# Some modulation chunks of a two-block transformer kernel go from TensorE to VectorE, with a TensorE sum over partitions one step later

## The chip, the cores and the metric

One core of a Trainium2 chip runs the whole program in one launch. The time is the device time of that core in microseconds, from the first instruction to the last; lower is better.

## What is computed

Batch 1, 256 tokens, width 1024, all in float32. `first_block` has two layers, each with a token mixer (sparse attention over an index, forgetting attention, two gated branches) and a convolutional FFN of inner width 2816. `second_block` adds two layers of five gated branches. Only the modulation of the first block matters here:

```python
for l in range(DEPTH):                      # DEPTH = 2
    mod = c @ mod_w[l] + mod_b[l]           # c: 1 x 1024, mod_w[l]: 1024 x 6144
    sh1, sc1, g1, sh2, sc2, g2 = [m[:, None, :] for m in jnp.split(mod, 6, axis=-1)]
    h = _rmsnorm(x, norm1_g[l]) * (1.0 + sc1) + sh1
    x = x + g1 * _mixer(h, ...)
    h = _rmsnorm(x, norm2_g[l]) * (1.0 + sc2) + sh2
    x = x + g2 * _conv_ffn(h, w_up[l], conv_w[l], conv_b[l], w_down[l])
```

Each `mod` is a row vector times a 1024 x 6144 matrix: six groups g of 1024 columns, cut into four parts of 256 columns. A chunk is one such part, 1024 x 256 weights, 1 MB. Two layers have 48 chunks.

## The kernel before

**Planning.** `plan()` writes a list of steps in one order. Each engine goes through this same list and issues what it has to do for each step, so the list is at once the order of every engine's queue. Weights come as 1 MB chunks through a ring of five buffers (`RING`), one DMA each on SP's queue; SP waits for the chunk five places earlier to be released. A weight chunk has two blocks of eight 128 x 128 tiles. ScalarE copies each block to `w_hi` (L1649, rounded to fp32r), VectorE writes the rest `w_lo` (L2042), and TensorE makes three products per tile: L1351, L1352, L1357 (L1389, L1390, L1395 for token-major outputs). There are six slots for split blocks (`SPLIT`). `split_to(upto)` on ScalarE and `split_to(behind)` on VectorE (one block fewer) stand ahead of each step's own work.

**A modulation chunk on TensorE** (`mod`, L1435): eight float32 matmuls with a 128 x 32 stationary operand, in four column groups, so that four partial rows arise at partitions 0, 32, 64 and 96. ScalarE copies them to `modacc` (L1698). With part 3 of a group, ScalarE writes the four rows of the group to HBM (`mod_rows`, L1703); `modload` reads them back feature-major (L1710), waiting first for the write to have arrived; `modsum` on VectorE (L2047, L2144) adds the four rows and the bias.

**A modulation chunk on VectorE** exists for two chunks at the start (`first_mod` with by_vector): eight chained instructions over 128 x 256 (L2119, L2121, L2122), each scaling by one column of `c` and adding to `modacc`. What is left, a sum over 128 partitions, is done there by small matmuls (`modred`).

**Who calls.** `some_mod()` first calls `reduce_mod()` (which adds `modsum` for a group already loaded, then `modload` for a group just completed) and then takes one chunk from the queue, in the order g = 2, 4, 3, 5 of layer 0 and g = 0, 1, 2, 4, 3, 5 of layer 1. In layer 0 it is called twice in the projections, once after the fox queries, after each odd gate tile (`gate1`, j = 1 to 15), after each of the first y1 groups as long as the next chunk isn't of g = 5, after odd `up` steps, and after each of the eight outputs `dn` of the down projection. `gap_mod()` puts one chunk on either side of the norm that follows. In the step list of layer 0 the chunks are: (4,3) after gate j = 9, then (3,0), (3,1), (3,2) after j = 11, 13, 15 and (3,3) in y1; (1,2,0) ahead of the down projection, then (1,2,1) to (1,2,3), (1,4,0) to (1,4,3), (1,3,0) after dn 0 to dn 7, and (1,3,1), (1,3,2) around the norm of layer 1.

**The down projection.** `dn` j takes 22 tiles (66 matmuls); VectorE then adds the bank to x (L2413), ScalarE squares x (`stat`, L1683). After the last one TensorE sums the squares (L1413, L1416), `root` takes the logarithm and exponent on ScalarE (L1688, L1690), and VectorE finishes the root and the norm.

**Sparse attention next to the gates.** `tp` turns the probabilities, which VectorE and ScalarE copy in turn out of the bank (L2355, L1843); `pv` (L1526) multiplies with the values; `no` (L2363, L2047) divides on VectorE; `lg` (L2328) is VectorE's pass over the next tile's logits.

## Time and profile before

| | |
|---|---|
| three runs | 1539.85, 1541.74, 1541.89 us; median 1541.74 |
| the profiled execution | 1542.8 us, of which the span is 1541.0 us |
| TensorE busy | 1496.3 us, 97% |
| VectorE busy | 1143.7 us, 74% |
| ScalarE busy | 833.4 us, 54% |
| mean granted TensorE clock | 0.993 |
| DMA | 290.5 MB, mean 189 GB/s |

In the profile PE is TensorE (PEld its weight loads), DVE VectorE, ACT ScalarE, POOL GpSimd, SP SyncE. L12 is line 12 of the kernel. In a timeline row stand start, duration, engine, line, operation, output and inputs, and in brackets the idle time ahead of it with what ended it; durations of TensorE matmuls overlap, so their starts are to be read.

### The profile page before, as it was taken

How to read it: one execution, taken by the hardware profiler on the slowest of the kernel's cores; microseconds unless marked ns; L12 is line 12 of the kernel's file. 1: busy time of each engine (PE TensorE's matmuls, PEld its weight loads, DVE VectorE, ACT ScalarE, POOL GpSimd, SP SyncE). 2: the span in 40 equal slices, each digit the busy share in tenths (PEclk: the TensorE clock that was granted, in tenths of full speed). 3: DMA queues.
4: the chain of work that ended last, by engine and by line, in shares of the span. 5: the costliest groups of instructions: out<-in, count | busy, mean ns of one | idle time of the engine just before them, and what ended most of it. 6: DMA issues, size and time to landing. Idle time of an engine off the chain costs nothing.

```text
span 1541.0 us, 31309 instructions
## 1 busy us (share of the span) xinstructions
PE 1496.3 (97%) x12608; PEld 1433.5 (93%) x12608; DVE 1143.7 (74%) x2202; ACT 833.4 (54%) x1509; POOL 31.4 (2%) x36
## 2 busy tenths in 40 slices
PE   6999999999999999999999999999999999999997
PEld 4898898999998999989999989999999999999997
DVE  5758566888646586769996678878966988888774
ACT  3655545655435646446555655645555754645453
POOL 0000001000000000010001000000000000000000
PEclk9999999999999999999999999999999999999998
DMA  9654555676776452454545543443446444444430
GB/s 393 251 216 184 202 223 192 219 275 247 275 272 252 168 214 87 157 196 165 179 179 194 219 164 113 169 185 138 154 152 246 150 154 163 167 163 141 169 129 28
DMA packets 47840, 290.51 MB, mean 189 GB/s; under 512 B 9992, under 2 KB 12296, under 8 KB 13136
## 3 DMA queue, kind: packets, MB, share of 16 engines
q1 hardware_dynamic: 38880, 280.83, 49.0%
q10 hardware_dynamic: 8816, 7.67, 1.5%
q8 instruction: 101, 1.65, 0.4%
q14 instruction: 43, 0.35, 0.1%
HBM read 286.09 MB, written 2.39 MB: 187 GB/s over the span
## 4 chain that ended last, share of the span: by engine, by line
PE 57%; DVE 1%; ACT 1%; DMA 0%; issue 0%; DVEq 0%; ACTq 0%
PE bank L1351 17%; PE bank L1357 16%; PE bank L1352 16%; PE bank L1601 2%; PE sums L1526 1%; PE sums L1416 1%; PE bank L1390 1%; PE bank L1395 1%; PE bank L1389 1%; PE bank L1508 1%; PE bank L1499 1%; DMA mem_x<-mem_t 0%; DVE w_lo L2042 0%; ACT w_hi L1649 0%; PE bank L1533 0%
## 5 line engine op out<-in xcount | busy, mean ns | idle before, releaser
L1351 PE MATMUL bank<-h_hi,w_hi 128*128 128x256 f32 x2256 | 632.8, 288 | 8.9 <-ACT h_hi L1746 3.7
L1352 PE MATMUL bank<-h_hi,w_lo 128*128 128x256 f32 x2256 | 622.3, 283 | 0.0
L2042 DVE TENSOR_TENSOR w_lo<-ring,w_hi 128x1024 fp32r<-128x1024 f32 x436 | 523.4, 1222 | 106.4 <-ACT w_hi L1649 103.8
L1357 PE MATMUL bank<-h_lo,w_hi 128*128 128x256 f32 x2256 | 575.9, 283 | 0.0
L1649 ACT ACTIVATE w_hi<-ring 128x1024 fp32r<-128x1024 f32 x436 | 449.2, 1054 | 131.4 <-PE bank L1357 130.9
L1351 PEld LDWEIGHTS bank<-h_hi,w_hi 128*128 128x128 f32 x2256 | 432.8, 192 | 22.9 <-issue 17.9
L1352 PEld LDWEIGHTS bank<-h_hi,w_lo 128*128 128x128 f32 x2256 | 433.0, 192 | 0.6 <-issue 0.5
L1357 PEld LDWEIGHTS bank<-h_lo,w_hi 128*128 128x128 f32 x2256 | 405.2, 192 | 0.0
L1351 PE MATMUL bank<-a_hi,w_hi 128*128 128x256 f32 x352 | 99.6, 283 | 1.0 <-DVE w_lo L2042 0.7
L1352 PE MATMUL bank<-a_hi,w_lo 128*128 128x256 f32 x352 | 98.3, 279 | 0.0
L1357 PE MATMUL bank<-a_lo,w_hi 128*128 128x256 f32 x352 | 98.2, 279 | 0.0
L1389 PE MATMUL bank<-w_hi,h_hi 128*128 128x256 f32 (+1 forms) x304 | 86.6, 289 | 3.9 <-ACT h_hi L1746 2.9
L1390 PE MATMUL bank<-w_lo,h_hi 128*128 128x256 f32 (+1 forms) x304 | 85.7, 286 | 0.0
L1883 ACT ACTIVATE conv_a<-bank,sm 128x256 f32<-128x256 f32 x44 | 24.8, 564 | 105.2 <-PE bank L1357 105.2
L1395 PE MATMUL bank<-w_hi,h_lo 128*128 128x256 f32 (+1 forms) x304 | 81.7, 287 | 0.0
L1351 PE MATMUL bank<-y_hi,w_hi 128*128 128x256 f32 x288 | 79.3, 280 | 0.0
L1352 PE MATMUL bank<-y_hi,w_lo 128*128 128x256 f32 x288 | 78.8, 278 | 0.0
L1357 PE MATMUL bank<-y_lo,w_hi 128*128 128x256 f32 x288 | 75.7, 281 | 0.0
L1944 ACT ACTIVATE sig<-bank 128x256 f32<-128x256 f32 x80 | 30.3, 379 | 78.1 <-PE bank L1357 77.5
L1351 PEld LDWEIGHTS bank<-a_hi,w_hi 128*128 128x128 f32 x352 | 66.1, 188 | 4.7 <-issue 3.3
L1389 PEld LDWEIGHTS bank<-w_hi,h_hi 128*128 128x128 f32 x304 | 59.6, 196 | 7.2 <-issue 5.9
L1352 PEld LDWEIGHTS bank<-a_hi,w_lo 128*128 128x128 f32 x352 | 66.2, 188 | 0.0
(336 smaller groups left out, 2345.7 us busy)
## 6 DMA issues: line engine op xcount, KB each, us to landing
ring<-weights SPq DMA_DIRECT2D x266, 1024.0 KB, 4.9
pos_bias<-scratch ACTq DMA_DIRECT2D x4, 512.0 KB, 5.6
x<-x_t ACTq DMA_DIRECT2D x1, 1024.0 KB, 6.9
scratch<-line ACTq DMA_DIRECT2D x1, 1024.0 KB, 5.6
mem_x<-mem_t ACTq DMA_DIRECT2D x1, 1024.0 KB, 6.7
mem_second<-mem_t ACTq DMA_DIRECT2D x1, 1024.0 KB, 6.2
out_t<-x SPq DMA_DIRECT2D x2, 512.0 KB, 2.6
co<-const SPq DMA_DIRECT2D x1, 462.0 KB, 7.2
```

Of the source, the lines that this page charges most:

```text
L1351: pe.matmul(to, WH[:, b % SPLIT, o, :], hi[:, k, :], start=(i == 0), stop=False)
L1352: pe.matmul(to, WL[:, b % SPLIT, o, :], hi[:, k, :], start=False, stop=False)
L1357: last = pe.matmul(to, WH[:, b % SPLIT, o, :], lo[:, k, :], start=False, stop=(i == n - 1))
L1389: pe.matmul(o, q, WH[:, s:s + m.n, k, :], start=(k == 0), stop=False)
L1390: pe.matmul(o, q, WL[:, s:s + m.n, k, :], start=False, stop=False)
L1395: last = pe.matmul(o, q, WH[:, s:s + m.n, k, :], start=False, stop=(k == KD - 1))
L1416: m = pe.matmul(sums[:, 0:S], ones, hb[:, k, :], start=(st.n is None and k == 0), stop=(k == KD - 1))
L1601: m = pe.matmul(to[:, (2 * g + s) * P:(2 * g + s + 1) * P], k[half, g, s * P:s * P + P], q[half, g, t * P:t * P + P], start=True, stop=True)
L1649: act.activation(WH[:, b % SPLIT], ring_half(b), ACT.Copy).then_inc(w_hi, 1)
L1883: act.activation(to[:, st.j % 3, :], bank[u.bank][:, 0:S], ACT.Identity, scale=ss(("conv_w", st.l, 2), c), bias=ss(("conv_b", st.l), c)).t ...
L1944: act.activation(sig2[:, st.j % 4, :], bank[st.ps.bank][:, 0:S], ACT.Tanh, scale=0.5).then_inc(taken[st.ps.bank], 1)
L2042: ve.tensor_tensor(WL[:, b % SPLIT], ring_half(b), WH[:, b % SPLIT].bitcast(F32), ALU.subtract).then_inc(w_lo_v, 1)
```

## The change

`some_mod()` gets a flag by_vector. It is set after gate tiles with j > 8 of layer 0, and after dn with j < 6 of layer 0. A chunk taken with the flag is made by VectorE as eight chained instructions, and takes no bank and no step of TensorE. The sum over the 128 partitions follows in a new step `modrow`, which `some_mod()` puts into the list at its next call, ahead of the next chunk: one float32 matmul with a 128 x 128 block of ones, so that every partition holds the sum, and ScalarE copies it to `modacc` scaled by 0.25 (four rows of it are added later). When the row completes a group, `some_mod()` returns without taking a chunk. VectorE now also waits ahead of such a chunk for the previous group's rows to have been written to HBM. In the diff the three engine parts at the end are TensorE's, ScalarE's and VectorE's, in this order.

```diff
+BY_VECTOR = 6
...
+    def mod(l, g, part, by_vector=False):
         p.chunks.append(("mod", (l, g, part)))
-        st = p.add("mod", chunk=len(p.chunks) - 1, l=l, g=g, part=part, ps=p.full_bank(),
-                   n=p.count("mod_rows") if part == 3 else p.counts.get("mod_rows", 0), after=state["parts"])
+        n = p.count("mod_rows") if part == 3 else p.counts.get("mod_rows", 0)
+        more = dict(v=p.count("mod_v"), eng="vector") if by_vector else dict(ps=p.full_bank(), after=state["parts"])
+        st = p.add("mod", chunk=len(p.chunks) - 1, l=l, g=g, part=part, n=n, **more)
+        if by_vector:
+            state["row"] = st
+            return
         state["parts"].append(st.ps)
         if part == 3:
             state["summed"] = (l, g)
+
+    def mod_row():
+        st, state["row"] = state["row"], None
+        if st:
+            row = p.add("modrow", l=st.l, g=st.g, part=st.part, n=st.n, v=st.v, ps=p.full_bank(), after=state["parts"])
+            state["parts"].append(row.ps)
+            if st.part == 3:
+                state["summed"] = (st.l, st.g)
...
-    def some_mod(n=1):
+    def some_mod(n=1, by_vector=False):
         reduce_mod()
+        mod_row()
+        if state["summed"]:
+            return
         for _ in range(min(n, len(queue))):
             l, g, part = queue.pop(0)
-            mod(l, g, part)
+            mod(l, g, part, by_vector)
...
     def gap_mod():
-        if queue and not state["summed"]:
+        if queue and not state["summed"] and not state["row"]:
             mod(*queue.pop(0))
...
             if j % 2 and queue and queue[0] > (0, 9, 9) and len(queue) > 4 or j % 2 and l == 0:
-                some_mod()
+                some_mod(by_vector=l == 0 and j > 8)
...
             if queue and queue[0][1] != 5:
                 some_mod()
+            else:
+                mod_row()
...
             ps = fm("dn", dn[j], j=j, l=l).ps
-            some_mod()
+            some_mod(by_vector=l == 0 and j < BY_VECTOR)
...
+            def modrow(st):
+                to = claim(st.ps)
+                pe.wait_ge(mod_v, st.v + 1)
+                pe.matmul(to[:, 0:256], ones, modacc[:, st.part, :], start=True, stop=True).then_inc(ready, 1)
...
+            def modrow(st):
+                wait_ready(act, st.ps)
+                act.activation(modacc[:, st.part, :], bank[st.ps.bank][:, 0:256], ACT.Copy, scale=0.25).then_inc(
+                    taken[st.ps.bank], 1)
+                if st.part == 3:
+                    for u in st.after:
+                        wait_taken(act, u)
+                    act.dma_start(mod_rows.ap()[st.n], modacc[0:97:32, :, :]).then_inc(mod_row_out, 16)
...
             def mod(st):
                 if st.eng != "vector":
                     return
+                if st.n is not None:
+                    ve.wait_ge(mod_row_out, 16 * st.n)
```

## Rows read from the trace of the kernel before

**Rows 1.** Profile page: busy time by engine, share of the span, instructions.
```profile
PE 1496.3 (97%) x12608; PEld 1433.5 (93%) x12608; DVE 1143.7 (74%) x2202; ACT 833.4 (54%) x1509; POOL 31.4 (2%) x36
```

**Rows 2.** Timeline of PE around a modulation chunk of the down projection.
```profile
438.41 0.28 PE L1357 MATMUL bank<-a_lo,w_hi 128*128 128x256 f32 x1
438.62 1.07 PE L1435 MATMUL bank<-ring,c_wide 128*32 128x256 f32 x16
439.62 0.39 PE L1351 MATMUL bank<-a_hi,w_hi 128*128 128x256 f32 x1
```

**Rows 3.** Timeline of PE at the root: float32 sums with ones, two records a matmul.
```profile
466.32 0.70 PE L1413 MATMUL sums<-mean,co 128*128 128x256 f32 x2
466.85 0.59 PE L1416 MATMUL sums<-h_val,co 128*128 128x256 f32 x2
```

**Rows 4.** Timeline of DVE at the start: one modulation chunk by VectorE.
```profile
13.40 0.35 DVE L2119 TENSOR_SCALAR modacc<-ring,sm 128x256 f32<-128x256 f32 x1 [4.42 <-DMA ring<-weights]
17.31 0.15 DVE L2047 TENSOR_TENSOR modv<-bank,sm 128x2 f32<-128x2 f32 x1
```

**Rows 5.** Timeline of DVE beside the gates, 167 to 176 us.
```profile
167.29 0.19 DVE L2363 RECIPROCAL stats<-stats 128x8 f32<-128x8 f32 x1
170.01 0.69 DVE L2047 TENSOR_TENSOR o_tm<-sums,stats 128x512 f32<-128x512 f32 x1 [2.53 <-PE sums L1526]
171.09 0.69 DVE L2047 TENSOR_TENSOR o_lo<-bank,o_hi 128x512 fp32r<-128x512 f32 x1 [0.38 <-ACT o_hi L1854]
...
175.40 0.42 DVE L2355 COPY probs_t<-bank 128x256 f32<-128x256 f32 x1
```

**Rows 6.** Timeline of PE, same place: last gate matmul, first `pv`.
```profile
175.56 0.28 PE L1357 MATMUL bank<-h_lo,w_hi 128*128 128x256 f32 x1
175.97 0.52 PE L1526 MATMUL sums<-v_a,probs_t 128*128 128x64 f32 x3
```

**Rows 7.** Timeline of DVE: the longest idle beside gate j = 13; ahead of wo1.
```profile
195.36 0.69 DVE L2047 TENSOR_TENSOR o_tm<-sums,stats 128x512 f32<-128x512 f32 x1 [4.58 <-PE sums L1526]
...
234.88 0.48 DVE L2408 SCALAR_TENSOR_TENSOR x<-bank,modv,x 128x256 f32<-128x256 f32 x1 [5.42 <-PE bank L1357]
```

**Rows 8.** Timeline of DVE in the down projection, dn 3 to dn 5.
```profile
438.73 0.48 DVE L2413 SCALAR_TENSOR_TENSOR x<-bank,modv,x 128x256 f32<-128x256 f32 x1 [5.01 <-PE bank L1357]
...
441.40 0.81 DVE L2047 TENSOR_TENSOR modv<-modv 128x16 f32<-128x16 f32 x2
...
448.10 3.48 DVE L2042 TENSOR_TENSOR w_lo<-ring,w_hi 128x1024 fp32r<-128x1024 f32 x3
```

**Rows 9.** Timeline of ACT: row write at dn 6; copy and root behind dn 7.
```profile
459.92 0.50 ACTq L1703 DMA_DIRECT2D mod_rows<-modacc  x1
460.46 0.42 ACT L1683 ACTIVATE h_val<-x 128x256 f32<-128x256 f32 x1 [0.65 <-ACT modacc L1698]
...
468.34 0.36 ACT L1698 ACTIVATE modacc<-bank 128x256 f32<-128x256 f32 x1
...
470.23 0.47 ACT L1688 ACTIVATE guess<-sums,co 128x256 f32<-128x256 f32 x1 [0.91 <-PE sums L1416]
```

**Rows 10.** DMA queues in 463.92:464.42, 4.0 to 4.5 us after that row write's issue.
```profile
q10 hardware_dynamic: 1, 0.00, 0.1%
```

**Rows 11.** DMA queues in 168.38:168.88, 1.0 to 1.5 us after an earlier row write's issue.
```profile
q10 hardware_dynamic: 8, 0.02, 12.3%
```

**Rows 12.** Windows of 2 us: stretch, busy PE, PEld, DVE, ACT, POOL, PEclk, DMA share, GB/s.
```profile
476.00:478.00 2.00, 2.00 (x11) 2.00 (x11) 2.00 (x7) 1.18 (x3) 0.00 (x0) 0.50 1.00 422
...
680.00:682.00 2.00, 1.57 (x13) 1.60 (x14) 1.82 (x6) 1.17 (x4) 0.00 (x0) 1.00 1.04 438
```

**Rows 13.** Timeline of PE: its work after idle at two norms.
```profile
469.06 1.13 PE L1416 MATMUL sums<-h_val,co 128*128 128x256 f32 x4 [1.61 <-ACT h_val L1683]
...
474.05 0.36 PE L1389 MATMUL bank<-w_hi,h_hi 128*128 128x256 f32 x1 [2.00 <-ACT h_hi L1746]
...
680.43 0.36 PE L1351 MATMUL bank<-h_hi,w_hi 128*128 128x256 f32 x1 [1.86 <-ACT h_hi L1746]
```

More of the change, by code:

```diff
@@ L188, in plain @@
         return p.matrix([tile_cols(name, lead, [(c0 + P * j, P)], rows) for j in range(n)])
-    state = dict(parts=[], summed=None, loaded=None, added={}, all_by_pe={})
-    def mod(l, g, part):
+    state = dict(parts=[], summed=None, loaded=None, added={}, all_by_pe={}, row=None)
+    def mod(l, g, part, by_vector=False):
         p.chunks.append(("mod", (l, g, part)))
-        st = p.add("mod", chunk=len(p.chunks) - 1, l=l, g=g, part=part, ps=p.full_bank(),
-                   n=p.count("mod_rows") if part == 3 else p.counts.get("mod_rows", 0), after=state["parts"])
+        n = p.count("mod_rows") if part == 3 else p.counts.get("mod_rows", 0)
[4 more added lines that the diff above has]
+            return
         state["parts"].append(st.ps)
@@ L1625, in from_h @@
                 linear([(claim(st.ps)[:, 0:S], st.subs)], XH, XL)
-            do = dict(bias=bias, root=root, norm=norm, mem_again=mem_again, mod=mod, modred=modred, tm=tm, tr=tr,
+            do = dict(bias=bias, modrow=modrow, root=root, norm=norm, mem_again=mem_again, mod=mod, modred=modred, tm=tm, tr=tr,
                       cum=cum, idx=idx, qkf=from_h, gate1=from_h, lg=lg, tp=tp, pv=pv, ot=ot, y1=y1, wo1=wo1, up=up,
@@ L2010, in hgn @@
                 act.activation(hb[:, 6:8, :], hb[:, 6:8, :], ACT.Exp, scale=-0.5).then_inc(hg_guess, 1)
-            do = dict(setup=setup, bias=bias, mod=mod, modload=modload, stat=stat, root=root, norm=norm, mem_again=mem_again, load_mem=load_mem, tm=tm, decay=decay, idx=idx, tr=tr, decay2=decay2,
+            do = dict(setup=setup, bias=bias, mod=mod, modrow=modrow, modload=modload, stat=stat, root=root, norm=norm, mem_again=mem_again, load_mem=load_mem, tm=tm, decay=decay, idx=idx, tr=tr, decay2=decay2,
                       qkf=qkf, gate1=gate1,
```

## The prediction

> **What bounds the kernel now.** I began with the page's busy times: TensorE is busy 97% of the span, VectorE 74% [rows 1]. So a microsecond taken from TensorE's queue is a microsecond won, as long as nobody makes TensorE wait; and VectorE has 26% to give, if the free time lies where the work is put. The questions are local: how long TensorE spends on one modulation chunk, how long VectorE would, and what ends VectorE's idle time in the two stretches that the change touches. For these I read the timelines of PE and DVE there, then ACT and the DMA queues at the end of the down projection, because the change also moves the steps that follow a chunk.
>
> **How many chunks.** Following `some_mod` through the new code, not all flagged calls take a chunk. At the gates, j = 9 takes (4,3) by VectorE. At j = 11 its row is added, the group is complete, and the call returns without a chunk. j = 13 and 15 take (3,0) and (3,1). That is three, not four. In the down projection dn 0, 1, 2 take (2,1), (2,2), (2,3) of layer 1, dn 3 adds the last row and returns, dn 4 and 5 take (4,0) and (4,1): five, not six. Eight chunks are moved, and each return shifts all later chunks by one place: (3,2) and (3,3) of layer 0 are made by TensorE during y1; at dn 6 and dn 7 stand (4,2) and (4,3) by TensorE; and one chunk of g = 5 slides into the up stage of layer 1.
>
> **TensorE's side.** A chunk occupies it from 438.41 + 0.12 (the pitch of the matmul before) to the next start at 439.62: 1.09 us [rows 2]. The new row is a float32 matmul of 128 x 128 on 128 x 256. The trace has that very form, the sums at the root: from 466.32 to 466.85, 0.53 us [rows 3]; with 0.09 us for the change of kind, as ahead of 438.62, it is 0.62 [rows 2]. I take 0.575. So 8 x (1.09 - 0.575) = 4.1 us less, with 3.8 and 4.5 as its ends.
>
> **VectorE's side.** One chunk takes from 13.40 to 17.31, 3.91 us [rows 4].
>
> *Down projection.* After each dn VectorE adds to x, splits two or three blocks (three take 3.48 us), now and then does `modsum`, and then waits 5.0 us for TensorE [rows 8]. With the chunk it needs 0.40 + 3.42 + 3.91 = 7.7 us where three blocks are split; TensorE's period becomes 66 x 0.1165 + 0.575 = 8.3 us. It fits with half a microsecond to spare, and the row of each chunk, which TensorE asks for after the next dn, is there in time. Only after dn 5 there is `modsum` too (from 441.40 to about 442.4, 0.95 us): 8.7 us against 8.2, so the row of (4,1) holds TensorE for 0.45 us. Bounds: 0 (the splits can run ahead), 1.5 (0.3 at each of five rows). The ring buffer of a VectorE chunk is released some 6 us later than now, and SP's loads queue behind it; I placed the loads one by one and each still lands before its split, so nothing there.
>
> *Gates.* Here the chunk (4,3) comes right ahead of the reciprocal at 167.29, so it runs from there to 171.20. Queued behind it on VectorE are the reciprocal and the division `o_tm`, now at 170.01 after an idle of 2.53 [rows 5]: it would start at 171.45, 1.44 late. The idle of 0.38 and what else the semaphores cost ahead of `o_lo` at 171.09 takes some back, leaving 0.97. From there to the copy of the probabilities at 175.40 VectorE has no idle time, and that copy is just what TensorE needs at 175.97: the last gate matmul starts at 175.56, so 0.29 us of the gap is already a wait [rows 6]. TensorE would arrive 1.09 earlier and leave 0.97 later. The saving of this chunk is gone and 0.97 lost on top; as a stall beyond the TensorE sum it is 0.97 + 1.09 = 2.05 us. Bounds: 0.6 (if the logit passes catch up 1.4 us more) and 3.0. (3,0) falls into the idle of 4.58 us ahead of 195.36 [rows 7] and costs nothing. (3,1) delays the first y1 sums by some 2.5 us; TensorE's own chunks (3,2), (3,3) give that back by the third y1 pair, and ahead of the first sum of wo1 VectorE is idle for 5.42 us [rows 7]. Nothing.
>
> **What moves at the end of the down projection.** Today the last rows of group (1,4) are written with dn 6, at 459.92 [rows 9], and loaded behind dn 7, one period of 8.9 us later; by then the write has arrived. In the new plan (4,3) is made after dn 7, so its row write and, right behind the last squares, its `modload` stand on ScalarE's queue ahead of the logarithm of `root`. `modload` first waits for the write to have arrived. Queued behind it: L1688 and with it VectorE's root, the norm of layer 1 and TensorE. In the time of the old trace: the copy at 468.34, the write issued at 468.82, the squares 0.75 later (0.65 us of idle as at 460.46), so TensorE's sum would let the logarithm start at 470.98 instead of 470.23. It starts when both this and the load's issue are done. How long does a row write take? Ten are in the trace. With the queues nearly empty all eight packets moved 1.0 to 1.5 us after the issue [rows 11]; with weights filling them, which is the state at the end of the down projection, the last packet of the write at 459.92 moved 4.0 to 4.5 us after it [rows 10]. With 4.3: 468.82 + 4.3 + 0.4 for the load's issue = 473.5, against 470.23 now: 3.3 us. `modsum`, 0.95 us [rows 8], no longer stands ahead of VectorE's root, and I take a quarter of a microsecond back for it: 3.0 us. Bounds: 0.5 (write in 1.25 us; then only the late squares count) and 5.0 (write in 6.3 us, behind three loads).
>
> The rule on this is in the Trainium skill, DMA: Bandwidth & Descriptors, in its part on the fixed cost: about 2 us for any DMA, mostly the receipt of the write. Taken as it stands the logarithm would be 0.7 us late instead of 3.0. This trace disagrees where the queues are full [rows 10].
>
> **The sum.** -4.1 (TensorE) + 2.05 (gates) + 0.45 (row after dn 5) + 3.0 (root of layer 1) = +1.4 us. The chunk that slides into the up stage is in the count already. Added to the median, 1541.74 + 1.4 = 1543.1 us; the profiled run, 1542.8 with a span of 1541.0, would become about 1544.2 with a span of 1542.4. The difference of span and median is 0.7 us, which is in the range.
>
> **The rivals.**
>
> 1. *The forecast, +1.4.* For it: the place on ScalarE's queue is certain, the DMA state is that of [rows 10]. Chance 0.46.
>
> 2. *The write is quick.* Loads are issued later than now because ring buffers are held longer, and the write meets a gap. Then the root costs 0.5 to 0.7 and the sum is -1.0: 1540.7 us. Against it: the loads delayed by VectorE's last chunk bunch just there. The page's 2 us for a DMA is this case. Chance 0.17.
>
> 3. *All of VectorE's work hides and the write is quick:* -4.1 + 0.5 = -3.6, 1538.1 us. It needs the gate stretch to have slack that I don't see in [rows 5, 6]. Chance 0.10.
>
> 4. *The write waits behind the loads (slower).* At the root three chunks of 1 MB are due at once, since the buffers of (4,1), (4,2) and (4,3) come free within a few microseconds. If the write arrives more than 6 us after its issue, the root costs 4.7 or more and the sum passes +3.1; at 7.5 us it is +4.6: 1546.3 us. For it: the ring is fuller than today. Chance 0.17.
>
> 5. *The clock falls beside the gates.* TensorE would idle there for 0.97 + 1.09 + 0.29 = 2.3 us in one piece. After 1.86 us of idle, at 680.43, the granted clock stayed at 1.00, 2.4 GHz; after 1.61 and, a few microseconds later, 2.00 us of idle at the root of layer 1 it was 0.50, 1.2 GHz, for some 2.6 us [rows 12, 13]. If it falls here too, half of 2.6, 1.3 us, is lost: +2.7, 1544.4 us. The Trainium skill has this rule in TensorE: Matmul & The Clock Gate, in its part on oscillation: idle gaps put the clock to half. At the root the clock falls already, so a longer idle there costs little more. Chance 0.10.
>
> That the plan moves ten chunks and not eight would be -1.0 more; the code speaks against it, and it is in the width.
>
> **How the numbers follow.** What the measurement can tell from no change is about 0.2%, 3.1 us: below 1538.7 is faster, above 1544.8 slower. Rival 3 and the best end of 2 are faster: 0.10. Rival 4, and the worse end of 1 and 5, are slower: 0.24. The rest, 0.66, is the same. Range: from -2.8 (rivals 2 and part of 3) to +5.0 (rival 4 almost whole), 1538.9 to 1546.7.
>
> **What the profile after would show.** Right: 8 groups of L2122's kind more on VectorE and a new PE line with 16 float32 records; 64 matmuls, 128 records, fewer at the chunk line; an idle of 2.3 us of PE ahead of the `pv` behind gate j = 10, ended by the copy of VectorE; VectorE idle of about 0.5 us per dn where 5.0 stood; ScalarE idle for 2 to 3 us ahead of the logarithm behind the last dn of layer 0, and PE idle there of about 5 us instead of 2.00. Wrong: no idle at either place; a wait for `w_lo` or for weights' DMA inside the down projection, which would mean that the ring or VectorE is the bound; or the logarithm starting right after TensorE's sum.

## The result

The kernel after takes 1549.17 us, median of 15 runs (1543.94 to 1551.33), beside 1543.22 us for the kernel before in as many. The ratio is 1.0032, with an interval of 1.0023 to 1.0040: 3.5 to 6.2 us slower, 4.9 us at its middle; the two medians differ by 5.95 us. The forecast was +1.4 us and 1543.1 us, its range ended at 1546.7. So the sign was right, the size was not, and the time left the band that was called "the same". Of the 6.1 us between forecast and time, 1.5 us lie in the base: the forecast was added to 1541.74 us, the median of three runs, and fifteen runs of the kernel before give 1543.22.

The profiled execution of the kernel after took 1544.88 us (span 1543.1), one of its quickest; three further traces of it had spans of 1548.5, 1550.1 and 1551.1 us, two further ones of the kernel before 1542.7 and 1542.2.

Profile page of after, busy time by engine, beside [rows 1]:

```profile
PE 1492.4 (97%) x12496; PEld 1434.4 (93%) x12496; DVE 1174.7 (76%) x2266; ACT 832.6 (54%) x1509; POOL 31.6 (2%) x36
```

TensorE is busy for 3.9 us less and VectorE for 31 us more, as planned. TensorE's lines there, instructions, busy time and idle time before them:

```profile
L1459 PE MATMUL bank<-ring,c_wide 128*32 128x256 f32 x608 | 43.5, 411 | 14.5 <-DMA ring<-weights 14.5
L1448 PE MATMUL bank<-modacc,co 128*128 128x256 f32 x16 | 5.0, 393 | 1.0 <-DVE modacc L2157 0.9
```

Sixteen records of the new row step, two each, are eight moved chunks and not ten, as the prediction counted them.

**Beside the gates.** Timeline of PE in after; shown are the rows with idle time ahead of them, and a row step with its successor (the place of [rows 6]):

```profile
171.51 0.38 PE L1370 MATMUL bank<-h_hi,w_hi 128*128 128x256 f32 x1 [1.00 <-DVE o_lo L2080]
175.65 0.63 PE L1550 MATMUL sums<-v_a,probs_t 128*128 128x64 f32 x4 [1.00 <-DVE probs_t L2390]
179.22 0.60 PE L1448 MATMUL bank<-modacc,co 128*128 128x256 f32 x2
179.65 0.55 PE L1550 MATMUL sums<-v_a,probs_t 128*128 128x64 f32 x4
...
182.17 0.66 PE L1550 MATMUL sums<-v_a,probs_t 128*128 128x64 f32 x4 [1.35 <-ACT probs_t L1876]
```

Three waits, 3.35 us, where the kernel before has 0.13 us ahead of its first `pv` (175.56 + 0.28 to 175.97, [rows 6]) and 0.07 ahead of the third. In the whole stretch from 117 to 255 us TensorE is idle for 5.51 us, before for 2.36: 3.15 us more. Timeline of DVE ahead of the first two, beside [rows 5]:

```profile
169.54 0.48 DVE L2157 SCALAR_TENSOR_TENSOR modacc<-ring,sm,modacc 128x256 f32<-128x256 f32 x1
169.94 0.20 DVE L2398 RECIPROCAL stats<-stats 128x8 f32<-128x8 f32 x1
170.17 0.69 DVE L2080 TENSOR_TENSOR o_tm<-sums,stats 128x512 f32<-128x512 f32 x1
170.78 0.68 DVE L2080 TENSOR_TENSOR o_lo<-bank,o_hi 128x512 fp32r<-128x512 f32 x1
...
175.08 0.42 DVE L2390 COPY probs_t<-bank 128x256 f32<-128x256 f32 x1
```

The chunk (4,3) ends at about 169.9, and reciprocal, division and `o_lo` follow without idle time. The next gate tile needs the bank that `o_lo` reads: that is the first wait. Together with the second, ahead of `pv`, it is the idle time that was forecast as one piece of 2.3 us. The third was not forecast. Timeline of ACT:

```profile
180.64 0.38 ACT L1718 ACTIVATE modacc<-bank 128x256 f32<-128x256 f32 x1
181.12 0.51 ACTq L1723 DMA_DIRECT2D mod_rows<-modacc  x1
181.74 0.38 ACT L1876 ACTIVATE probs_t<-bank 128x256 f32<-128x256 f32 x1 [0.72 <-ACT modacc L1718]
```

The row's copy and the issue of the row write of group (4) stand on ScalarE's queue ahead of a copy of probabilities that TensorE is waiting for. In the kernel before, this write is issued some 14 us earlier, at 167.38 (its packets are [rows 11]). Not all of the 1.35 us is the write's: experiments 4 to 6 issue no write here, and a wait of 0.68 us stands at this place, because TensorE arrives earlier.

**Down projection and root.** Timeline of PE in after, the rows with idle time (beside [rows 2] and [rows 13]):

```profile
453.82 0.67 PE L1448 MATMUL bank<-modacc,co 128*128 128x256 f32 x2 [0.93 <-DVE modacc L2157]
455.13 1.07 PE L1459 MATMUL bank<-ring,c_wide 128*32 128x256 f32 x16 [0.64 <-DMA ring<-weights]
...
468.57 1.13 PE L1435 MATMUL sums<-h_val,co 128*128 128x256 f32 x4 [2.40 <-ACT h_val L1707]
...
471.97 1.07 PE L1459 MATMUL bank<-ring,c_wide 128*32 128x256 f32 x16 [1.27 <-DMA ring<-weights]
476.37 0.55 PE L1408 MATMUL bank<-w_hi,h_hi 128*128 128x256 f32 x1 [3.33 <-ACT h_hi L1779]
```

Timeline of ACT, same place (beside [rows 9]):

```profile
467.53 0.52 ACTq L1736 DMA_DIRECT2D mod_rows<-modacc  x1
468.10 0.72 ACT L1707 ACTIVATE h_val<-x 128x256 f32<-128x256 f32 x2 [0.68 <-ACT modacc L1731]
472.39 0.36 ACTq L1743 DMA_DIRECT2D modv<-mod_rows  x1
472.80 0.47 ACT L1712 ACTIVATE guess<-sums,co 128x256 f32<-128x256 f32 x1 [3.98 <-DMA mod_rows<-modacc]
```

Row write, squares, `modload`, logarithm, in the order that the prediction read out of the plan. The write is issued at 467.53, the load could go at 472.39: 4.86 us, and 5.20, 5.25 and 5.15 us in the other three traces of this kernel. The write's eight packets moved 3.5 to 5.0 us after its issue.

**Where the time goes.** The table has the time between starts of TensorE's matmuls behind idle times that both kernels have, in us, for all traces of the two. The first matmul of layer 0 comes at 33.8 to 36.2 us in all of them.

| stretch of TensorE | before (3 traces) | after (4 traces) |
|---|---|---|
| layer 0 to the first logits of the forgetting attention (117 us) | 81.70, 82.66, 82.08 | 81.88, 82.00, 83.10, 83.10 |
| to the second norm (255 us): gates, y1, wo1 | 138.09, 139.59, 138.08 | 139.24, 139.23, 140.72, 140.72 |
| to the sums of the root (469 us): up, down | 214.05, 215.53, 214.04 | 213.69, 214.34, 214.21, 214.15 |
| root of layer 1 (474 us) | 4.99, 4.99, 4.99 | 7.80, 8.16, 8.19, 8.10 |
| to 551 us | 76.90, 75.42, 76.90 | 77.50, 77.00, 76.93, 77.12 |
| to the second norm of layer 1 (680 us) | 129.48, 129.49, 129.46 | 129.49, 130.99, 130.99, 130.97 |
| to the second block's first norm (894 us) | 213.92, 213.43, 212.98 | 212.99, 212.99, 214.45, 215.53 |
| to the end | 646.65, 646.60, 647.52 | 646.75, 647.79, 646.73, 646.74 |
| sum | 1505.8, 1507.7, 1506.1 | 1509.3, 1512.5, 1515.3, 1516.4 |

The same step of about 1.5 us turns up in many lines, in both kernels. It is TensorE's clock. Windows of 2 us around the second norm (stretch, busy PE, PEld, DVE, ACT, POOL, PEclk, DMA share, GB/s), first of after:

```profile
254.00:256.00 2.00, 1.12 (x9) 1.15 (x10) 1.82 (x6) 1.33 (x3) 0.00 (x0) 0.97 1.00 422
256.00:258.00 2.00, 2.00 (x11) 2.00 (x11) 2.00 (x6) 1.15 (x4) 0.00 (x0) 0.50 1.03 434
258.00:260.00 2.00, 2.00 (x14) 2.00 (x13) 1.90 (x5) 1.43 (x4) 0.00 (x0) 0.68 1.00 410
```

and of the kernel before, in its third trace:

```profile
256.00:258.00 2.00, 1.69 (x14) 1.72 (x15) 1.90 (x5) 1.17 (x4) 0.00 (x0) 1.00 1.00 422
258.00:260.00 2.00, 2.00 (x19) 2.00 (x19) 2.00 (x6) 1.33 (x3) 0.00 (x0) 1.00 1.02 430
```

Behind the same idle of 1.86 us the granted clock is 0.50, 1.2 GHz, in the one and 1.00, 2.4 GHz, in the other. Such a fall costs 1.5 to 1.7 us over work, and it comes or stays away from execution to execution.

### The profile page after: what moved, and what is told of

The parts are those of the page before. It is cut to its first block, busy times and chain, and to the rows that moved or that the text cites. A ratio compares the mean times of both kernels' runs of the same rounds, so it can differ in the third digit from the quotient of the medians.

```text
span 1543.1 us, 31154 instructions
## 1 busy us (share of the span) xinstructions
PE 1492.4 (97%) x12496; PEld 1434.4 (93%) x12496; DVE 1174.7 (76%) x2266; ACT 832.6 (54%) x1509; POOL 31.6 (2%) x36
## 4 chain that ended last, share of the span: by engine, by line
PE 58%; DVE 2%; ACT 1%; issue 0%; DVEq 0%; ACTq 0%
PE bank L1370 17%; PE bank L1376 16%; PE bank L1371 16%; PE bank L1625 2%; PE sums L1550 1%; PE sums L1435 1%; PE bank L1409 1%; PE bank L1414 1%; PE bank L1408 1%; PE bank L1532 1%; PE bank L1523 1%; DVE w_lo L2075 0%; PE bank L1557 0%; PE bank L1638 0%; DVE macc L2080 0%
```

## The experiments

All medians are of 5 to 15 runs each unless a single run is named; a ratio is that to the kernel before on the same chip, with its interval, and 0.1% is 1.5 us. A "+3.5 us" is worked out from the ratio and can differ from the difference of two medians.

**1. The kernel after once more**, unchanged.

> The changed kernel again, unchanged, for a second trace. Its fifteen times fell into two groups, 1544 to 1545.5 us with a mean granted clock of 0.991 to 0.995, and 1549 to 1551 us with 0.988 to 0.992. Theory A (the clock of TensorE): the second group differs from the first by a longer stretch at 1.2 GHz, some 9 to 10 us more at half clock for 4.6 us lost, at one place where TensorE has just idled; the root of layer 1 is the candidate (0.5 from 474 to 480 us in the first trace). A trace of the second group then shows PEclk 0.5 in more windows and otherwise the same rows. Rival B (DMA): the second group waits longer for weights or for the row write, PEclk as before. A trace of 1544 to 1545 us again would tell neither.

1550.33 us, 1.0044 (1.0031 to 1.0057). The loss is real. Its trace has the same three waits beside the gates, 1.31 us of waiting for weights at 458 us, and 17.1 us of time lost to the clock before 1520 us, counted as the length of each 2 us window times (1 - PEclk); the first trace of after has 8.5, those of before have 6.8, 10.2 and 10.3. Theory A is the nearer one, though not at one place: more clock is lost than in the first trace near 30 us, at the root and near 900 us, and the clock also falls at 558 us. The third and fourth traces lost 15.4 and 17.1 us.

**2. Only the three chunks beside the gates.**

```diff
-BY_VECTOR = 6
+BY_VECTOR = 0
```

> The changed kernel with the flag off in the down projection; three chunks beside the gates by VectorE remain. Theory: the gates alone cost about 1.1 us (stalls of 1.0, 1.0 and 1.35 us of TensorE at 170 to 182 us against 3 x 0.5 saved), so ratio to before about 1.0007, and no wait for the row write at the root of layer 1. Rival (the gates carry the loss, by a clock that falls there in some runs): ratio 1.002 to 1.003 and two groups of times as with the whole change.

> Only the three chunks beside the last gates of layer 0 go by VectorE ((4,3), (3,0), (3,1)); all chunks of the down projection stay on TensorE. The run of the same kernel came out at 1548.64 us, 1.0032 of the kernel before, while its traced span shows only 3 stalls of 1.0, 1.0 and 1.35 us against 1.5 us saved. Theory A (the stalls are all there is, and the rest was the clock of few executions): the median lands near +1.5 to +2.5 us, ratio 1.001 to 1.0017. Theory B (the stalls beside the gates are followed by a lower granted clock or by waits for weights in a good part of the executions): +4 to +5.5 us again, ratio 1.0026 to 1.0036, and a trace with more than 8.5 us of clock lost before 1520 us or idle time of TensorE ended by weights in the down projection.

> One more execution of the kernel with only the three gate chunks by VectorE, for its trace. Its two traces so far had a wait for weights at 432 us (0.89 and 1.43 us) and 6.8 us of clock lost before 1520 us each, no more than the kernel before (6.8, 10.3 and 10.3). If the +4.7 us of its timed executions is clock lost near the gates in a part of them, one of its traces should sooner or later show a low clock between 160 and 260 us: here in about half the cases. If it shows none and again a wait for weights near 432 us, the waits behind the gates are the steady part of the loss and the clock's part stays open.

The edit takes the flag off the down projection, and the third of the three is a single run. 1548.64 us, 1.0032 (1.0020 to 1.0044), and again 1547.93 us, 1.0030 (1.0018 to 1.0042): +4.6 to +4.9 us where the forecast had 0.5 for these chunks (2.05 less 3 x 0.515). All three traces have the waits of 1.0, 1.0 and 1.35 us. In two of them the stretch from 117 to 255 us takes 1.14 us longer for it; in the second it takes 2.60 us longer, because TensorE also waits 1.40 us for weights at 217 us. Then there is a wait that nobody had on the list, in the down projection, where the steps and their order are those of the kernel before. Timeline of PE in its second trace:

```profile
434.33 1.07 PE L1459 MATMUL bank<-ring,c_wide 128*32 128x256 f32 x16 [1.43 <-DMA ring<-weights]
```

It is 0.89, 1.43 and 1.47 us. No ring buffer is released late here; the load itself is slow, 6.8, 7.3 and 7.4 us from issue to landing, where the same load takes 4.7 to 5.0 us in seven traces of kernels with the same steps there, the kernel before and experiments 3 and 4 among them. Why, the runs don't show. Together the steady waits are +2.0 to +2.6 us. The three traces take 4.0 us more than those of before on the mean, and that is 2.4 us of these waits, 0.5 for the wait at 217 us in one of three, and 1.1 us of clock. For the ratios, taken from other executions, the part of the clock isn't measured. In the third trace the clock is full beside the gates and 1.7 us are lost at 258 to 262 us, behind the second norm.

**3. Only chunk (4,3) beside gate 9.**

```diff
-                some_mod(by_vector=l == 0 and j > 8)
+                some_mod(by_vector=l == 0 and j == 9)
```

(and `BY_VECTOR = 0`)

> Only chunk (4,3) beside gate 9 of layer 0 goes by VectorE, its row added at j = 11; all others stay on TensorE, later chunks one place later. Theory A (the two stalls of 1.0 us behind it and the one of 1.35 us behind the row write are the whole loss of this place): 3.35 minus 0.52 saved, less 1.1 for the chunk that slides out of the gates into an idle place: +1.5 to +2.8 us, ratio 1.001 to 1.0018. Theory B (each stall there also brings a stretch of low clock): +3.5 to +5 us, ratio 1.0023 to 1.0032. If it comes out within 1 us of no change, the loss of the three-chunk version lies with (3,0) and (3,1).

1546.85 us, 1.0022 (1.0012 to 1.0032): +3.4 us. The one chunk brings all three waits. It was also expected that a chunk slides out of the stretch; it doesn't, (3,3) is made in y1 either way. Without that term the waits give 3.15 - 0.71 = +2.4 us (0.71 by experiment 5). In the trace the stretch to 255 us takes 142.26 us: that is +2.4 and a fall of the clock at 118 to 124 us. Its root of layer 1 is 1.0 us longer too, 5.99 us, though the steps there are those of before: VectorE waits 0.90 us for the load of group (1,4), which lands 5.6 us after its issue. The ratio lies between A and B, and the interval reaches into both.

**4. No chunk (4,3) beside the gates**, that is (3,0), (3,1), (3,2) at j = 11, 13, 15, and none in the down projection.

```diff
-                some_mod(by_vector=l == 0 and j > 8)
+                some_mod(by_vector=l == 0 and j > 10)
```

(and `BY_VECTOR = 0`)

> Beside the gates alone, j = 11, 13, 15 by VectorE, chunk (4,3) by TensorE, the down projection as before the change. Theory: the stalls of 1.0, 1.0 and 1.35 us come from chunk (4,3) and its row, so they are gone, and three swaps save 1.5 us: ratio 0.999, mean 5 to 6 us below that of the gates-only kernel. Rival (the extra 4 us of the gates-only kernel over what its trace shows are chance or from somewhere else): the difference of the means is 1.1 + 1.5 = 2.6 us.

1543.97 us, 1.0001 (0.9989 to 1.0013). The waits of 1.00, 1.00 and 1.35 us are gone (one of 0.68 is left), and so are the wait for weights at 432 us and the loss of experiment 2; the gain of 1.5 us that was expected lies within the interval but isn't shown.

**5. No group's last part by VectorE, so no call returns empty and nothing is shifted.** Eight chunks, as in after.

```diff
-                some_mod(by_vector=l == 0 and j > 8)
+                some_mod(by_vector=l == 0 and j > 10)
...
-            some_mod(by_vector=l == 0 and j < BY_VECTOR)
+            some_mod(by_vector=l == 0 and j < BY_VECTOR and queue[0][2] != 3)
```

> The change with the last part of each group left to TensorE: beside the gates the flag holds for j > 10, in the down projection for chunks of parts 0 to 2. Again eight chunks go to VectorE, but no call returns without a chunk, so every later chunk, row write and load stands where it stood before the change, and VectorE has none between gate tiles 9 and 10. Theory (the loss is from where the moved steps stand, not from VectorE's work as such): no stall at 170 to 182 us, no wait of the logarithm for the row write, 8 x 0.5 us saved, some 3 to 4 us under before, ratio 0.9975 to 0.9985. Rival (VectorE's work in itself costs, through the ring or the splits): ratio at or above 1.000.

1542.92 us, 0.9999 (0.9990 to 1.0008): the 5 us are gone, but the gain of 2 to 4 us that was expected isn't there. The stretch of the gates takes 136.56 us, 1.53 less than 138.09, though TensorE is idle in it for 2.97 us instead of 2.36, by a wait of 0.68 us for a copy of ScalarE: (1.53 + 0.61) / 3 = 0.71 us saved by a chunk. The rest of the gain ends in the down projection. Timeline of PE, rows with idle time:

```profile
436.35 0.67 PE L1448 MATMUL bank<-modacc,co 128*128 128x256 f32 x2 [0.77 <-DVE modacc L2157]
...
455.49 1.78 PE L1459 MATMUL bank<-ring,c_wide 128*32 128x256 f32 x16 [1.62 <-DMA ring<-weights]
```

The matmuls behind the second wait take 1.78 us where they take 1.07 elsewhere: the granted clock is 0.50 at 456 to 458 us, and another 1.7 us are lost. At the root TensorE's chunk waits 2.01 us for its weights, in the place of the idle time of 2.00 us.

**6. Six chunks: as 5, but in the down projection only up to dn 3.**

```diff
-            some_mod(by_vector=l == 0 and j < BY_VECTOR)
+            some_mod(by_vector=l == 0 and j < 4 and queue[0][2] != 3)
```

> A version that keeps only the chunks with idle time of VectorE around them and with no row write in the way: (3,0), (3,1), (3,2) beside the last gates, (2,1), (2,2), (4,0) in the down projection, six in all, each group's last part on TensorE, so nothing is shifted at the root. Saved: 6 x 0.515 = 3.1 us. Theory A (the loss of the eight-chunk variant without shifts, 0.9999, came from the waits for weights at the end of the down projection, 1.62 and 2.01 us, because the last ring buffers were held by VectorE): ratio 0.9975 to 0.9990. Theory B (what TensorE saves is given back at the next idle place or by the clock, whatever the chunks): 0.9995 to 1.0010.

1541.71 us, 0.9987 (0.9978 to 0.9995): 0.8 to 3.4 us faster than the kernel before, the only one here whose interval lies below 1. Its trace has no wait for weights in the down projection, only the wait of 0.78 us for VectorE's chunk at 434.97. Up and down take 213.12 us, 0.93 less, with 2.70 us of idle time instead of 1.78: (0.93 + 0.92) / 3 = 0.62 us saved by a chunk. That the ring buffers held late are the difference to 5 fits the two traces; two chunks fewer are moved as well, and the two aren't told apart.

**7. Only the down projection's chunks.**

```diff
-                some_mod(by_vector=l == 0 and j > 8)
+                some_mod()
```

> The changed kernel with the flag off beside the gates; five chunks in the down projection by VectorE remain. Theory: the down projection saves 1.1 us by its end, the root of layer 1 then costs 3.6 (the logarithm behind the arrival of the row write), so 1.5 to 2.5 us over before in the trace; if the two groups of times belong to the root, they are here too and the ratio is 1.0015 to 1.003. Rival (the loss is at the gates): ratio at or below 1.000.

1546.10 us, 1.0019 (1.0010 to 1.0027), +2.9 us; with experiment 2 the parts give 7.5 us, against 4.9 and 6.8 us for the whole. Up and down take 211.99 us, 2.06 less than 214.05: just the forecast -5 x 0.515 + 0.45 = -2.1, though by other terms: -5 x 0.62, +0.94 for the row behind dn 5, +0.42 for weights, +0.79 for late squares and -1.09 for the chunk that leaves the stretch are -2.0 (all below). The root takes 8.15 us, as in after.

**8. Only the shift, no work for VectorE.** The kernel before; behind dn 3 of layer 0 no chunk is taken.

```diff
-            some_mod()
+            if l or j != 3:
+                some_mod()
```

> The kernel before with every chunk on TensorE; the only edit: no chunk is taken behind dn 3 of layer 0, so each later chunk stands one place later, and the row write of group (1,4) and its load stand on ScalarE's queue ahead of the logarithm of the root of layer 1, as in the kernel after. No VectorE work, no other saving. Theory A (the root is the place of the loss, and the clock makes it more): layer 1 starts 2.5 to 3.6 us later by the idle time alone, less 0 for savings (the one chunk slides into the up stage), and the granted clock at the root stays low for longer, 1.7 us more: +3 to +5 us, ratio 1.002 to 1.0034. Theory B (the wait costs only what the idle time shows, the clock falls there in any case): +2 to +3.2 us, ratio 1.0013 to 1.002. Theory C (without the late loads of VectorE's chunks the write arrives quickly): under +1 us, ratio below 1.0007.

1547.14 us, 1.0023 (1.0013 to 1.0033), +3.5 us. Shifting steps, with nothing else changed, costs 3.5 of the whole change's 4.9 us. Timeline of ACT:

```profile
470.07 0.50 ACTq L1704 DMA_DIRECT2D mod_rows<-modacc  x1
470.62 0.72 ACT L1684 ACTIVATE h_val<-x 128x256 f32<-128x256 f32 x2 [0.66 <-ACT modacc L1699]
475.03 0.40 ACTq L1711 DMA_DIRECT2D modv<-mod_rows  x1
475.47 0.47 ACT L1689 ACTIVATE guess<-sums,co 128x256 f32<-128x256 f32 x1 [4.13 <-DMA mod_rows<-modacc]
```

4.96 us from write to load without any late buffer of VectorE. The root takes 7.97 us.

**9. The same shift, with the load behind the root.** The call of `reduce_mod()` that followed the down projection of layer 0 now stands in `norm`, behind `root(...)`.

```diff
             root(i, kind)
+        if late_load:
+            reduce_mod()
         if mods:
...
         x_stats = stats([], "x", down)
-        reduce_mod()
+        if l == L1 - 1:
+            reduce_mod()
```

> The kernel with the shifted chunks and no VectorE work (1.0023), with one more edit: the load of group (1,4) stands behind the root of layer 1 on ScalarE's queue, so nothing at the root waits for the row write. If the wait for the write is the loss: the excess falls from 3.6 us to 0 to +1 us, ratio 0.9998 to 1.0007, and the idle times at the root are 1.6 and 2.0 us again. Rival (the later squares and the chunk shifted into the root are the loss): +2 to +3.5 us, ratio 1.0013 to 1.0023.

1543.11 us, 1.0004 (0.9995 to 1.0013). ACT:

```profile
471.96 0.50 ACTq L1707 DMA_DIRECT2D mod_rows<-modacc  x1
472.51 0.72 ACT L1687 ACTIVATE h_val<-x 128x256 f32<-128x256 f32 x2 [0.66 <-ACT modacc L1702]
474.14 0.47 ACT L1692 ACTIVATE guess<-sums,co 128x256 f32<-128x256 f32 x1 [0.91 <-PE sums L1420]
474.65 0.42 ACT L1694 ACTIVATE guess<-guess 128x256 f32<-128x256 f32 x1
477.68 0.36 ACTq L1714 DMA_DIRECT2D modv<-mod_rows  x1
478.14 0.38 ACT L1702 ACTIVATE modacc<-bank 128x256 f32<-128x256 f32 x1 [3.08 <-DMA mod_rows<-modacc]
478.42 0.90 ACT L1750 ACTIVATE h_hi<-h_val,modv 128x256 fp32r<-128x256 f32 x2
```

The write took even longer, 5.72 us. The logarithm doesn't wait for it any more and starts when TensorE's sum is there. But the load still holds ScalarE's queue: the copy `h_hi` of the norm starts 1.87 us after VectorE's `h_val` (476.55, timeline of DVE), against 0.52 us in the kernel before (472.88 and 473.40), and the root takes 6.08 us against 4.99. The squares are 0.8 us late (an idle of 2.38 where 1.61 was). The chunk that slides out of the stretch saves 1.1 us, so +0.8 us is left, and the ratio gives +0.6. Here the trace is that of the slowest of eleven runs, 1548.67 us, with 15.3 us of clock lost; the place is read from it, not the time. So most of the loss at the root is the load's wait for the write ahead of the logarithm; the rival, late squares and the shift as such as the whole loss, has fallen.

**10. The kernel after with that load behind the root.**

> The whole change, but the load of group (1,4) stands behind the root's logarithm and exponent on ScalarE's queue instead of ahead of them. Theory (the wait for the row write costs 3 us at the root, and sets off the longer stretch at half clock): the logarithm starts as soon as TensorE's sum ends, about 2.5 us earlier, the idle of TensorE ahead of layer 1 goes from 3.3 back to about 1 to 2 us, and the time falls by 2.5 to 3 us, to a ratio of about 1.0005 to 1.001 to before, in one group of times. Rival: the norm waits for something else (the row write only hid it), and the time stays within 1 us of the whole change.

1546.33 us, 1.0022 (1.0011 to 1.0032), against 1.0032 and 1.0044 of after; the intervals overlap, so it is the trace that shows the gain. The idle ahead of the norm's first matmul falls from 3.33 to 1.17 us, the root from 8.06 (mean of four) to 5.68. The gates' 1.14 us are left, and 0.69 at the root, where the load waits for the write as in 9; the rest of the +3.4 us isn't located.

**11 and 12. The price of idle time at the root by itself.** The kernel before; two and then six copies of the sums on ScalarE ahead of the logarithm, chained by a semaphore.

```diff
+                if st.i == 2:
+                    for i in range(2):
+                        act.activation(guess[:], sums[:, 0:S], ACT.Copy).then_inc(delayed, 1)
+                        act.wait_ge(delayed, i + 1)
```

> The kernel before, with two more operations of ScalarE (a copy of the sums, chained by a semaphore, some 0.5 us each as the logarithm is) ahead of the logarithm of the root of layer 1; nothing else. It prices idle time of TensorE at this place by itself: about 1.0 us more. Theory A (a longer idle there makes a second stretch of low clock more likely): the time is 1.5 to 3 us up, ratio 1.001 to 1.002. Theory B (the idle costs itself alone): +1.0 us, ratio 1.0004 to 1.0009.

> As the kernel with two added operations of ScalarE ahead of the logarithm of the root of layer 1, but six: about 3.0 us more of idle time of TensorE, as the forecast had it for the kernel after. Theory A (the long idle costs a further stretch of low clock): +4.5 to +5.5 us, ratio 1.003 to 1.0036, and the trace shows 3.4 us of clock lost or more between 460 and 490 us instead of 1.7. Theory B (the idle costs itself alone): +3.0 us, ratio 1.0017 to 1.0022, 1.7 us of clock lost there.

Two: 1546.46 us, 1.0015 (1.0005 to 1.0025), +2.3 us; the trace has 0.58 us more idle time there, and the stretch behind it is as long as before. Six: 1545.64 us, 1.0023 (1.0010 to 1.0037), +3.5 us. The idle in its trace is 4.24 us instead of 2.00, so 2.24 us more, and the stretch behind it is another 1.02 us longer. Windows of six:

```profile
474.00:476.00 2.00, 0.00 (x0) 0.00 (x0) 1.59 (x4) 0.90 (x3) 0.00 (x0) 1.00 1.06 446
476.00:478.00 2.00, 0.68 (x3) 0.71 (x4) 1.78 (x5) 0.91 (x2) 0.00 (x0) 0.55 0.96 406
478.00:480.00 2.00, 2.00 (x11) 2.00 (x11) 2.00 (x7) 1.31 (x3) 0.00 (x0) 0.50 1.05 442
480.00:482.00 2.00, 2.00 (x12) 2.00 (x11) 2.00 (x7) 1.23 (x3) 0.00 (x0) 0.50 0.97 410
```

The clock is low from 476 us on for nearly three windows; in the trace of before only the one of [rows 12], 476 to 478 us, is wholly low, those on either side have 0.77 and 0.88. Part of it lies over the idle, where it costs nothing; what lies over work costs the 1.0 us. So a longer idle does cost more than itself, though less than expectation A had it. The two intervals overlap, and the smaller one leaves +0.8 to +3.9 us for 0.58 us of idle: that the medians carry more than the traces show is true of this run too, and isn't explained by it.

**13. More traces**, a single run each: two of the kernel before, two of after.

> The kernel before, unchanged, for a second trace. Theory (the granted clock falls at a fixed set of places, at 30, 256, 474, 556 and 896 us, each in a part of the executions that depends on where the kernel starts): this trace shows one at 256 or 556 us, or the same two as the first with a start elsewhere. Rival (only the changed kernel falls at 256 and 556): none there.

> The kernel before, for a third trace; as the one ahead of it.

> The kernel after once more, for its trace. From the first matmul of layer 0 to the end it took 1509.3 and 1512.5 us in its two traces so far, the kernel before 1505.8, 1507.7 and 1506.1. If the loss at the root is steady: 2.6 to 3.2 us more between the first sum and the first h matmul of layer 1 than the 4.99 us of before, again, and a low clock in its work there. If the rest is chance: the stretch from 117 to 257 us takes 139.2 us, that from 257 us to the sums 212.0 us plus 0 or 1.7 us of clock. A total under 1508 us would mean that most of the 5 us is not in every execution.

> As the run before it, for a fourth trace of the kernel after. Steady parts: 139.2 us in the gate stretch (138.1 in before), 7.8 to 8.2 us at the root (4.99). Chance parts: 1.7 us of clock near 118, 257 and 556 us, 1.7 or 3.4 near 897 us. The mean of the four totals should stand 4 to 5.5 us above the mean of before (1506.5) if traces and timed executions tell the same; a mean under +3 would leave a loss that the traces do not show.

With the first traces and that of experiment 1 they are the columns of the table. The falls of the clock are not the same set each time: the first trace of before has one at 474 us and none at 118 and 258, the second has those two and none at 474. The root's 7.8 to 8.2 us is steady, as is 139.2 in the stretch of the gates, plus 1.5 where the clock fell. The mean of the four totals is 1513.4 us, 6.9 above before's 1506.5, somewhat more than the 4 to 5.5 expected: the traces show the whole loss.

Over all twenty traces, the clock fell behind the idle of 1.86 us at the second norm of layer 0 in 7 of the 8 whose kernel has the three gate chunks with (4,3), and in 2 of the 12 others. That idle is the same in all. It goes with the gate chunks; by which way, these runs don't tell.

## Why the prediction was wrong

Four steps of the sum failed on the dear side: the row write on ScalarE's queue beside the gates, which was left out (the term is low by 1.1 us); the weight loads of the down projection, put at nothing (1.07 us); the length of the write at the root (low by 0.9 us); and the clock, held at its old level everywhere (2.0 us, argued only). Two steps failed the other way: TensorE's saving was 1.0 us larger, and the chunk that slides away, which the sum did not list, gave 1.1 us. The sum had four terms. In their place stand six, from the traces, each against the kernel before:

| term | forecast | measured |
|---|---|---|
| TensorE, 8 chunks | -4.1 | -5.1 (3 x 0.67 + 5 x 0.62) |
| waits beside the gates | +2.05 | +3.15 (5.51 - 2.36 of idle time) |
| row after dn 5 | +0.45 | +0.93 |
| wait for weights behind it | 0 | +1.07 (0.64, 1.31, 1.18, 1.14) |
| root of layer 1 | +3.0 | +3.9 (8.06 - 4.99, and 0.80 at the squares) |
| chunk that slides into layer 1's up stage | in the count | -1.1 |
| sum, paid in every execution | +1.4 | +2.9 |
| clock | 0 | the rest of 4.9 us, 2.0; not measured by itself |

The 0.67 is TensorE's busy time in the stretch of the gates, 135.73 us before and 133.73 after, by three chunks. That the rest of 2.0 us is clock is argued and not shown: in the traces of after 8.5 to 17.1 us of clock are lost, in those of before 6.8 to 10.3, but no run changes the clock by itself.

**How many chunks: right.** Eight, with the two empty calls in their places. So was what followed from it: the shift brings the largest single cost.

**TensorE's side: right in kind, low.** 0.62 to 0.71 us are saved by a chunk, and 5.1 us lie outside the ends that were given, 3.8 and 4.5. The pitch of the row step is 0.43 us beside the gates (179.22 to 179.65); the estimate from [rows 3] with 0.09 for each change of kind, 0.62, was too high, and 0.575 still was.

**The chunk that slides into the up stage: an omission.** It leaves the stretch ahead of the root (-1.09), and "in the count already" meant that it costs the same in the up stage. But there TensorE had waited 1.35 us for a `w_lo` at 699.53. In the traces of after this wait is gone, and the stretch takes 212.99 us at its best as it did before (212.98). It fills an idle place.

**Gates: the mechanism was right, the account of who waits was not.** VectorE's chunk did delay `o_tm` and the copy of the probabilities, and the stall it makes was sized well: 1.00 + 1.00 - 0.13 = 1.87 us against 2.05. Only it comes in two pieces, because the gate tile in between needs the bank that `o_lo` empties. What failed is that the step followed VectorE's queue alone. The row write of the completed group goes out at j = 11, on ScalarE's queue, ahead of a copy that TensorE needs, and the wait there is 1.35 us, half of it TensorE's earlier arrival. At the root the prediction did follow the row write through ScalarE's queue, beside the gates it didn't.

**Down projection.** The row of (4,1) holds TensorE for 0.93 us; its bounds held that (0 to 1.5). That the loads cost nothing failed: a later chunk waits for its DMA for 1.07 us, in the kernel without shifts for 1.62. The load for the wait at 455.13 is issued at 447.92, 0.38 us behind another one (447.54), and as the second of the pair takes 7.1 us to land (7.6 to 7.7 in the other three traces of after). In the kernel before the load used behind dn 6 is issued as the first of its bunch, at 450.52, and lands in 4.8 us. So the loads come in other bunches than before; that buffers released late bunch them is likely and not shown, since the order of the loads moved too. The prediction had named "a wait for `w_lo` or for weights' DMA inside the down projection" as a sign of being wrong. Experiment 6, which takes VectorE off the late places, has neither the wait nor the loss. Experiment 2 shows that such a wait can also come from a slow load, so how much of the 1.07 us comes from buffers released late isn't fixed; with the gates' chunks left out it is 0.42 us (experiment 7).

**Root of layer 1: right in place, order and cause, low by 0.9.** 4.86 to 5.25 us from the write's issue to the load against an assumed 4.3 [rows 10]: that was the moment of the last packet, not of the release. TensorE also waits for the weights of its own chunk there (1.27 us), but inside the longer wait. A slip without effect: the kernel before issues its load at 465.74, 5.8 us behind the write and not 8.9. Rival 2, the quick write, falls here: 4.9 to 5.7 us in eight traces of five kernels, with the weight loads filling the queues. The Trainium skill gives about 2 us as the fixed cost of a DMA (DMA: Bandwidth & Descriptors, in the part on the anatomy of one DMA, fitted to DMAs that GpSimd issues); this trace does not agree for a small write on ScalarE's queue behind such loads. The 16 KB are no part of it: [rows 11] shows 1.0 to 1.5 us with light queues.

**"At the root the clock falls already, so a longer idle there costs little more": wrong in size, and asked at too few places.** A fall was priced at 1.3 us (half of 2.6); the windows of before give 1.7. Experiment 12 puts it at 1.0 us for 2.24 us more of idle. In after the root and the stretch behind it take 85.2 us, 3.3 more than 81.9, of which some 0.2 us can be clock, so this was not where most of it went. The larger error was to treat the clock as fixed at each place: low behind [rows 12]'s first idle, full behind the other. It isn't. Rival 5 had this mechanism, with a chance of 0.10 and its place beside the gates. There it never happened, in nine traces with those waits; it happened at 257 us, in four of four traces of after, at 558 us in three, at 118 and 690 us in two. The Trainium skill has the rule in TensorE: Matmul & The Clock Gate, in the part on oscillation, that idle gaps put the clock to half. These traces agree that a fall always follows one, and show that the same gap can be followed by either level.

**Chances and range.** Slower had 0.24, most of it for one mechanism, a write that takes over 6 us. It took 4.9 to 5.25. Four terms came 0.5 to 1.1 us dearer, two 1.0 and 1.1 us cheaper, and the clock is the likely rest. A range that adds the clock's own spread, 1.7 us at each of some six places where the schedule leaves TensorE idle, would have reached past 1549 us.

## What to carry to other kernels

When a plan shifts, follow the small steps, not the large ones: a 16 KB write whose reader stands ahead of a logarithm cost 3.5 us, most of what moving eight chunks of 1 MB did, and with the reader behind the logarithm the loss was no longer clear of noise (1.0004, 0.9995 to 1.0013), though the norm still waited 1.3 us for it. Before giving work to an engine with idle time, list every reader of every bank and buffer that it will hold longer, for each queue, and choose the places by that: six chunks placed so gained 2 us where eight lost 5. And in a kernel at 97% of TensorE, take two or three traces of the kernel before ahead of any forecast of this size: one trace shows one draw of the clock.

## What the runs showed of the hardware

- The granted clock behind equal idle times (1.13, 1.86, 2.00 us) is 1.00 in one execution of the kernel before and 0.50 in another; a fall costs 1.5 to 1.7 us where it lies over work, and nothing where it lies over idle time.
- A 16 KB row write to HBM on ScalarE's queue, while 1 MB weight loads fill the DMA engines, releases its waiter 4.9 to 5.7 us after the issue (eight traces); in after its packets move 3.5 to 5.0 us after the issue, against 1.0 to 1.5 us with light queues [rows 11].
- The same 1 MB weight load, in the same place of the step list, takes 4.7 to 5.0 us to land in seven traces and 6.8 to 7.4 us in the three of experiment 2.
- A float32 sum over partitions by a 128 x 128 block of ones on 128 x 256 costs TensorE 0.43 us from start to next start (179.22 to 179.65 in after), where the 128 x 32 chunk that it replaces costs 1.00 (179.63 to 180.63 in before).
